# A two-block transformer forward pass: the recurrence's q and f as seven products of halves, a third slot of modulation weights, pooling matmuls moved one stage on

## What is computed

```python
h = _layer_norm(x) * (1 + sc1[:, None]) + sh1[:, None]
proj = h @ w_in[l] + b_in[l]              # hq, hf, hi (values), hg (gate): 1024 columns each
...
f = lb + (1 - lb) * jax.nn.sigmoid(f_raw)
log_f = jnp.log(f); k = 1 - f
b = jnp.cumsum(lfc, axis=3)               # inside a chunk of 32 tokens
q_in = qc * jnp.exp(b); k_in = kc * jnp.exp(-b); k_end = kc * jnp.exp(b_last - b)
att = where(causal, q_in k_in^T, 0);  o_intra = att v
S = exp(b_last) * S + k_end^T v;      o_inter = q_in S
```

## Time and profile before

| What | Value |
|---|---|
| Runs | 1941.75, 1940.38, 1933.2 us; median 1940.38 us |
| Profiled execution | 1938.68 us, its span 1936.9 us |
| Mean granted TensorE clock | 0.958 |
| TensorE busy (matmuls) | 1715.1 us, 89% |
| VectorE busy | 765.1 us, 40% |
| ScalarE busy | 431.8 us, 22% |
| GpSimd busy | 103.2 us, 5% |
| DMA | 474.79 MB, mean 245 GB/s |

### The profile page before, as it was taken

The page is one execution under the profiler, slowest core; times in us unless marked ns, Lnnn a source line. Parts: engine busy times, 40 slices in busy tenths (PEclk is TensorE's granted clock), DMA queues, the critical chain, the costliest instruction groups (busy, mean ns, idle before and its releaser), DMA issues. The chain is left out here.

```text
span 1936.9 us, 21905 instructions
## 1 busy us (share of the span) xinstructions
PE 1715.1 (89%) x8024; PEld 975.1 (50%) x8024; DVE 765.1 (40%) x1907; ACT 431.8 (22%) x1072; POOL 103.2 (5%) x127
## 2 busy tenths in 40 slices
PE   6999999799998999998987887877799899898786
PEld 3656554366667888655332332322358554533232
DVE  6544445665556645364110111011545454321115
ACT  4223232105443000013110110101212340222121
POOL 1100000000000000000000000000000000011110
PEclk9999999889999999998999999999989999899899
DMA  8633325951110622545999999999512224699995
GB/s 354 240 149 108 140 98 200 348 215 53 42 73 23 261 88 87 228 204 228 408 428 428 426 427 427 425 428 419 209 44 71 89 93 201 253 405 426 424 422 214
DMA packets 69798, 474.79 MB, mean 245 GB/s; under 512 B 11566, under 2 KB 12782, under 8 KB 45760
## 3 DMA queue, kind: packets, MB, share of 16 engines
q1 hardware_dynamic: 52944, 398.66, 50.7%
q0 software_dynamic: 15600, 70.61, 9.5%
q10 hardware_dynamic: 1152, 4.19, 0.5%
HBM read 459.53 MB, written 34.11 MB: 255 GB/s over the span
## 5 line engine op out<-in xcount | busy, mean ns | idle before, releaser
L2181 PE MATMUL moe_ps<-moe_up,moe_hg 128*64 128x512 f32 x1536 | 371.5, 640 | 107.9 <-DMA moe_up<-in_exp_gate 39.2
L2181 PEld LDWEIGHTS moe_ps<-moe_up,moe_hg 128*64 128x64 f32 x1536 | 130.5, 147 | 345.3 <-issue 344.9
L2220 PE MATMUL moe_ps<-moe_down,moe_midT 128*64 128x512 f32 x720 | 161.1, 596 | 10.3 <-DMA moe_down<-in_exp_down 9.0
L532 PE MATMUL mx_pair<-hT,hg_w 128*128 128x512 f32 x336 | 147.8, 596 | 0.0
L2273 ACT ACTIVATE moe_sig<-moe_ps 128x512 f32<-128x512 f32 (+1 forms) x32 | 15.7, 491 | 534.2 <-PE moe_ps L2181 534.2
L2302 DVE COPY moe_midT<-moe_ps 128x512 f32<-128x512 f32 (+1 forms) x32 | 17.8, 558 | 283.7 <-PE moe_ps L2192 283.7
L2312 DVE SCALAR_TENSOR_TENSOR moe_res<-moe_ps,moe_route_slot_share,moe_gain 128x512 f32<-128x512 f32 x64 | 45.1, 747 | 155.2 <-PE moe_ps L2220 155.0
L2220 PEld LDWEIGHTS moe_ps<-moe_down,moe_midT 128*64 128x64 f32 x720 | 52.1, 137 | 98.6 <-issue 95.6
L2258 ACT ACTIVATE moe_hg<-moe_ps,mod,scale_ffn 128x128 f32<-128x128 f32 x248 | 89.9, 467 | 50.9 <-PE moe_ps L2164 50.9
L532 PEld LDWEIGHTS mx_pair<-hT,hg_w 128*128 128x128 f32 x336 | 62.7, 190 | 75.7 <-issue 74.9
L2294 DVE TENSOR_TENSOR moe_mid<-moe_sig,moe_ps 128x512 f32<-128x512 f32 (+1 forms) x32 | 17.8, 555 | 143.4 <-PE moe_ps L2181 140.5
(11 more groups left out here) (422 smaller groups left out, 2549.9 us busy)
## 6 DMA issues: line engine op xcount, KB each, us to landing
moe_down<-in_exp_down SPq DMA_DIRECT2D x44, 2048.0 KB, 33.9
moe_up<-in_exp_up SPq DMA_DIRECT2D x31, 2048.0 KB, 34.1
moe_up<-in_exp_gate SPq DMA_DIRECT2D x31, 2048.0 KB, 34.2
moe_up<-in_exp_in SPq DMA_DIRECT2D x31, 2048.0 KB, 33.0
rest_w<-in_mod_rest POOLq DMA_DIRECT2D x16, 1536.0 KB, 8.8
hg_w<-in_w_hg SPq DMA_DIRECT2D x32, 512.0 KB, 3.8
rest_w<-in_mod_rest POOLq DMA_DIRECT2D x8, 2048.0 KB, 8.5
xn<-in_w_merge SPq DMA_DIRECT2D x32, 512.0 KB, 4.3
```

Of the source, the lines that this page charges most:

```text
L532: last = pe.matmul(proj[bank][:, :], w[s][:, kc, :], k.hT[:, kc, :], start=(kc == 0), stop=(kc == KC - 1))
L2181: last = pe.matmul(self.up_ps[u][e * SLOTS:(e + 1) * SLOTS, :], self.hg[m % 2][:, kc, e * SLOTS:(e + 1) * SLOTS], w[:, kc, :], start=(kc = ...
L2220: last = pe.matmul(self.res_ps[side][e * SLOTS:(e + 1) * SLOTS, :], self.midT[:, f, e * SLOTS:(e + 1) * SLOTS], w[e][:, f, side * 512:(sid ...
```

## The change

Three parts.

1. **Recurrence.** For heads 1 to 7, q and f are made together as seven products of halves: the two slices are the rows of a 2x2 of weight blocks (q and f above each other, inner rows 0 to 3 and 4 to 7), hT is the other 2x2 (inner blocks, tokens 0 to 255 and 256 to 511). The seven results live in the two banks, two halves each (`part_a` to `part_d`). VectorE makes sums of hT once (`token_sums`), sums of weights for each head (`weight_sums`) and adds the results (`results`). The keys of the head before are turned between the fourth and the fifth product, and ScalarE keeps them first. `rest.multiply` moves from ahead of the loop over heads to the end of each head, so that batch n is multiplied in head n's body and batch 7 after the last chain. SyncE waits for the end of the products before it sends the next q and f.
2. **Modulation weights.** Room for nine blocks, three slots. Three groups are sent at the recurrence's end, after batch 7 was used, and the others as slots come free.
3. **Second block.** The pooling matmuls and their scaling leave `project_second`; they go into `forgetting` with a bank of their own, the first before unit 0 and the others in units 2, 4 and 6.

```diff
-        self.w = k.sb(ctx, "rest_w", [P, 6, D])
+        self.w = k.sb(ctx, "rest_w", [P, self.GROUP * self.SLOTS, D])
...
-                with sp.Fori(1, HEADS) as n:
+                def next_slices(n):
                     for s, a in enumerate(slices):
-                        sp.wait_ge(S["used_" + a], n)
+                        if s == 0 and not isinstance(n, int):
+                            sp.wait_ge(S["qf_done"], n - 1)
+                        elif isinstance(n, int) or s >= 2:
+                            sp.wait_ge(S["used_" + a], n)
                         sp.dma_start(w[s], w_hg[n, s]).then_inc(S["loaded_" + a], 16)
...
+                def project_qf(n, first):
                     pe.wait_ge(S["g_kept"], n)
                     pe.wait_ge(S["q_kept"], n)
-                    feature_major(0, "q", 0, n)
+                    pe.wait_ge(S["loaded_q"], n * 16 + 16)
+                    product(part_a, W.a11, B.b11, True)
+                    pe.wait_ge(S["sums2"], n)
+                    product(part_b, W.s2, B.t2).then_inc(S["p6_done"], 1)
                     pe.wait_ge(S["v_kept"], n)
-                    feature_major(1, "f", 1, n)
+                    pe.wait_ge(S["sums4"], n)
+                    product(part_c, W.s3, B.t3, True)
+                    product(part_d, W.s1, B.t1).then_inc(S["p5_done"], 1)
+                    turn_keys(n - 1, first)
+                    pe.wait_ge(S["u2_kept"], n)
+                    product(part_a, W.a12, B.b21).then_inc(S["p2_done"], 1)
+                    pe.wait_ge(S["c22_kept"], n)
+                    product(part_c, W.a22, B.t4)
+                    product(part_d, W.s4, B.b22).then_inc(S["qf_done"], 1)
...
-                    keep_qf(n + 1, False)
                     keep_keys(n)
+                    keep_qf(n + 1)
...
+                def weight_sums(n, first=False):
+                    for a in "qf":
+                        dve.wait_ge(S["loaded_" + a], n * 16 + 16)
+                    if not first:
+                        dve.wait_ge(S["qf_done"], n - 1)
+                    dve.tensor_tensor(W.s1, W.a21, W.a22, ALU.add)
+                    dve.drain()
+                    dve.tensor_tensor(W.s2, W.s1, W.a11, ALU.subtract).then_inc(S["sums2"], 1)
+                    dve.tensor_tensor(W.s3, W.a11, W.a21, ALU.subtract)
+                    dve.drain()
+                    dve.tensor_tensor(W.s4, W.a12, W.s2, ALU.subtract).then_inc(S["sums4"], 1)
+
+                def results(n):
+                    dve.wait_ge(S["p6_done"], n)
+                    dve.wait_ge(S["q_kept"], n)
+                    dve.tensor_copy(u2, part_a)
+                    dve.drain()
+                    dve.tensor_tensor(u2, u2, part_b, ALU.add).then_inc(S["u2_kept"], 1)
+                    dve.drain()
+                    dve.wait_ge(S["p5_done"], n)
+                    dve.tensor_tensor(u3, u2, part_c, ALU.add)
+                    dve.drain()
+                    dve.tensor_tensor(u3, u3, part_d, ALU.add).then_inc(S["c22_kept"], 1)
+                    dve.wait_ge(S["qf_done"], n)
+                    dve.tensor_tensor(c21, u2, part_c, ALU.add).then_inc(S["c21_ready"], 1)
+                    dve.tensor_tensor(c12, u2, part_d, ALU.add).then_inc(S["c12_ready"], 1)
+
+                def head(n, last=False):
+                    results(n + 1)
+                    masked_scores(n)
+                    forget(n + 1, False)
+                    chain(n)
+                    running(n + 1)
+                    if not last:
+                        weight_sums(n + 2)
+                    keep_values(n + 1, False)
+                    decayed(n + 1, False)
+                    rest.multiply(dve, n)
+
+                token_sums()
                 forget(0, True)
                 running(0)
                 keep_values(0, True)
+                weight_sums(1, True)
                 decayed(0, True)
-                rest.multiply(dve, 0)
...
                 masked_scores(HEADS - 1)
                 chain(HEADS - 1)
+                rest.multiply(dve, HEADS - 1)
...
                 pool.wait_ge(rest.used, HEADS)
-                for group in range(2):
+                for group in range(rest.SLOTS):
                     rest.load_second(pool, group)
...
-                for g in range(G):
-                    pe.matmul(ps[g][:, :], w_pool[:, g, :], diff[:, g, :], start=True, stop=True).then_inc(pooled, 1)
...
+                pooled(0)
                 for i in range(len(units)):
                     turn(i)
                     if i + 3 < len(units):
                         scores(i + 3)
                     if i:
                         mix(i - 1)
+                    if i in (2, 4, 6):
+                        pooled(i // 2)
...
+                    if i in (2, 4, 6, 8):
+                        keep_pooled(i // 2 - 1)
```

More of the change, by code:

```diff
@@ L196, in __init__ @@
         self.loaded = k.dma_sems["rest_loaded"]
-        self.second_loaded = [k.dma_sems[f"rest_second_loaded{s}"] for s in range(2)]
+        self.second_loaded = [k.dma_sems[f"rest_second_loaded{s}"] for s in range(self.SLOTS)]
         self.used = k.sem(ctx, "rest_used")
@@ L484, in recurrence @@
         one_lb = k.sb(ctx, "hg_one_lb", [P, HEADS])
+        sums_h = area[:, 18 * SEQ:24 * SEQ].rearrange("p (q k n) -> p q k n", q=3, k=4)
+        B = Halves(k.hT, sums_h, rest.free[:, 6:8, :].rearrange("p a n -> p (a n)").rearrange("p (k n) -> p k n", n=256))
+        W = WeightHalves(w[0:2], k.sb(ctx, "hg_w_sums", [P, 3, 4, P]))
+        qf_bias = k.sb(ctx, "hg_qf_bias", [P, 2])
+        u2, u3, c21, c12 = (rest.free[:, 4:6, :].rearrange("p a n -> p (a n)")[:, j * 256:(j + 1) * 256] for j in range(4))
+        part_a, part_b, part_c, part_d = (proj[j // 2][:, j % 2 * 256:(j % 2 + 1) * 256] for j in range(4))
         lb, v_bias = k.lb, k.value_bias[:, 0:D]
@@ L546, in project_gv, with project_v @@
                     project_v(n)
-                def project_v(n):
-                    pe.wait_ge(S["f_kept"], n + 1)
+                def project_v(n, read="c12_ready", times=0):
+                    pe.wait_ge(S[read], n + times)
                     pe.wait_ge(S["loaded_v"], n * 16 + 16)
@@ L563, in scores_and_updates @@
                     last.then_inc(S["keys_turned"], 1)
+                def scores_and_updates(n, first):
                     pe.wait_ge(S["qin_ready"], n + 1)
@@ L730, in _ @@
                 keep_values(0, True)
+                weight_sums(1, True)
                 decayed(0, True)
-                rest.multiply(dve, 0)
-                with dve.Fori(0, HEADS - 1) as n:
-                    forget(n + 1, False)
-                    masked_scores(n)
-                    chain(n)
-                    running(n + 1)
-                    keep_values(n + 1, False)
-                    decayed(n + 1, False)
-                    rest.multiply(dve, n + 1)
+                dve.wait_ge(k.dma_sems["bias_stored"], 16)
+                with dve.Fori(0, HEADS - 2) as n:
+                    head(n)
+                head(HEADS - 2, True)
                 masked_scores(HEADS - 1)
                 chain(HEADS - 1)
+                rest.multiply(dve, HEADS - 1)
             @block.gpsimd
@@ L879, in _ @@
             def _(pool):
-                for group in range(2, rest.GROUPS):
-                    pool.wait_ge(rest.second_used, group - 1)
+                for group in range(rest.SLOTS, rest.GROUPS):
+                    pool.wait_ge(rest.second_used, group - rest.SLOTS + 1)
                     rest.load_second(pool, group)
@@ L2956, in _, with forgetting @@
                         for g in range(2 * (n - 4), 2 * (n - 4) + 2):
-                            last = windowed(g)
-                last.then_inc(diff_ready, 1)
-                for g in range(G):
-                    dve.wait_ge(pooled, g + 1)
-                    dve.tensor_scalar(catT[:, 4 + g, :], ps[g][:, :], k.col("pool_scale_2", g), None, ALU.mult)
+                            windowed(g)
                 dve.drain()
-def forgetting(k, qk, v_tok, catT, send_next):
+def forgetting(k, qk, v_tok, w_pool, diff, catT, send_next):
     nc = k.nc
```

112 lines of the change are left out of this document (72 added, 40 removed).

## The result

The changed kernel takes 1947.15 us (median of nine runs, 1943.89 to 1948.35), the kernel before on the same chip 1938.65 us (nine runs, 1933.2 to 1941.75). The ratio is 1.0046, 95% interval 1.0035 to 1.0056: slower by 0.46%, just inside the bound of 0.5%. The forecast of 1928.5 us, with a range to 1938, was wrong in size and in sign. The profiled execution took 1948.35 us, its span 1946.2, clock 0.950.

What follows compares the result with a forecast made beforehand. The prediction took TensorE's queue to set the time of a head in the recurrence. Recurrence -15.1, modulation weights +0.5 and pooling +3.5 summed to -11.1 us, giving 1928.5 us, range 1920 to 1938.

Runs made afterwards that it cites:

- the batch in the hole of 4.5 us: Changed kernel with each modulation batch multiplied in VectorE's idle time between c22 and the seventh product's end, batch 7 at head 6's end: 1913.46 us, ratio 0.9877.
- the batch at its old place: Changed kernel with modulation batch 0 ahead of the loop over heads and batch n+1 at the end of head n's body, as before: 1926.67 us, ratio 0.9944.
- the late loads: Changed kernel with the first three modulation group loads moved from GpSimd's queue end in the recurrence to its start in the key stage: 1950.97 us, ratio 1.0069.
- two slots: Changed kernel with two slots for modulation weights instead of three, so two group loads at the recurrence's end: 1949.36 us, ratio 1.0065.

## What to carry to other kernels

When a step is moved, list who waits for the signal it gives, and in that queue what stands behind the wait: here an instruction that the critical engine needed stood behind a load that nobody was in a hurry for. Look for the place of a movable step among the idle stretches of its engine inside the loop, not at its ends; here the batch in the hole of 4.5 us was worth 13 us against the batch at its old place, at the end of the loop's body. A load that GpSimd sends ahead of a block's end should land before it. In a stage with full DMA engines, an added buffer gained only when it was filled before the stage.

## What the runs showed of the hardware

- The end of a block waited for DMAs that GpSimd's queue had sent, though no semaphore in the block asks for them: 13.9, 9.6 and 5.7 us in which no engine worked, until 2.4 to 3 us after the DMA engines were last full; 1.0 and 1.1 us where three loads were sent 16 to 17 us ahead and just landed; 0.3 to 0.4 us with no such load in flight. SyncE's loads were not tried so, and what it is in the block's end that waits, the profile doesn't show.
- TensorE's clock after a wait in the loop over heads: no fall behind twelve waits of 0.8 to 1.1 us for u2. Behind six waits of 2.2 to 2.3 us for k_end it fell twice in the changed kernel, once with the late loads and once with two slots. Behind the wait for the sums of weights in the first head it fell at 2.30 and 2.38 us and not at 2.33 and 2.52, and behind eight waits for u2 between 2.8 and 4.8 us it fell six times. A fall cost 1.4 to 1.8 us, and once 2.9. The tail shows it best: nine kernels, the one before among them, have the same wait of 1.93 us there for ScalarE (L653 of the kernel before), and the clock fell behind it in five and not in four, which is the 1.6 us between tails of 24.7 and 23.1. So the length of the wait alone doesn't decide.
